# Inverse norm roots as exp(-½ ln x) on ScalarE instead of a ScalarE root and a VectorE reciprocal

## The reference

```python
def rms_norm(x, g):
    xf = x.astype(jnp.float32)
    y = xf * lax.rsqrt(jnp.mean(xf * xf, axis=-1, keepdims=True) + NORM_EPS)
    return (y * g.astype(jnp.float32)).astype(x.dtype)
...
    for layer in range(DEPTH_2):
        x = x + mixers[layer](rms_norm(x, mix_norms[layer]))
        xn, mn, wq, wkv, wo = xattn[layer]
        x = x + memory_cross_attention(rms_norm(x, xn), rms_norm(mem, mn), wq, wkv, wo)
        fn, wg, wu, wd = ffns[layer]
        x = x + swiglu(rms_norm(x, fn), wg, wu, wd)
    return rms_norm(x, final_norm)
```

## Time and profile before

| | |
|---|---|
| median of the runs | 3710.95 us (3707.92 to 3712.61, 3 runs) |
| the profiled execution | 3723.11 us, span 3721.3 us |
| mean granted TensorE clock | 0.921 of full speed |
| PE busy | 3161.6 us, 85% |
| DVE busy | 2067.9 us, 56% |
| POOL busy | 1343.1 us, 36% |
| ACT busy | 715.0 us, 19% |
| DMA | 832.17 MB, 224 GB/s over the span |

### The profile page before, as it was taken

One profiled execution on the slowest core, in us unless ns is written; L12 is line 12 of the kernel. 1 busy time (PEld: TensorE's weight loads), 2 busy tenths in 40 slices (PEclk: granted clock), 3 DMA queues, 4 the chain that ended last, 5 costly groups with the idle time before them and its releaser, 6 DMA issues. The chain is left out here.

```text
span 3721.3 us, 45113 instructions
## 1 busy us (share of the span) xinstructions
PE 3161.6 (85%) x17286; PEld 2328.3 (63%) x17286; DVE 2067.9 (56%) x4210; ACT 715.0 (19%) x1731; POOL 1343.1 (36%) x1166
## 2 busy tenths in 40 slices
PE   8889988976778777567888988889988999999998
PEld 3566378742335343254677766667875788877787
DVE  2341355579898888677776687776444210133201
ACT  2231221121111111113210023210023210122100
POOL 0840032156777777643455555555300000000000
PEclk9998999988889998886899998899999899999999
DMA  6422100379999999976899999899820244422343
GB/s 213 128 74 77 40 3 16 96 273 360 368 364 367 380 385 375 365 260 196 305 333 390 394 369 323 301 351 385 304 82 26 77 133 150 147 91 77 116 147 102
DMA packets 420396, 832.17 MB, mean 224 GB/s; under 512 B 40467, under 2 KB 258510, under 8 KB 420174
## 3 DMA queue, kind: packets, MB, share of 16 engines
q0 software_dynamic: 147456, 536.94, 38.7%
q1 hardware_dynamic: 272726, 292.35, 24.0%
HBM read 827.02 MB, written 2.17 MB: 223 GB/s over the span
## 5 line engine op out<-in xcount | busy, mean ns | idle before, releaser
L2809 PE MATMUL banks<-arena 128*128 128x256 f32 (+1 forms) x4736 | 1079.3, 387 | 76.2 <-DMA arena<-in_l_w_up 27.0
L2809 PEld LDWEIGHTS banks<-arena 128*128 128x128 f32 (+1 forms) x4736 | 911.8, 194 | 229.8 <-issue 41.4
L2356 POOL DMA_INDIRECT arena<-in_peer_v,arena x512 | 584.1, 1141 | 414.4 <-DVE arena L2472 247.7
L2356 POOL DMA_INDIRECT arena<-in_peer_u,arena x512 | 569.9, 1113 | 442.5 <-DVE arena L2486 165.3
L2486 DVE CUSTOM_DVE_ANT_0 arena<-arena 128x1024 f32<-128x1024 f32 x512 | 628.0, 1227 | 109.2 <-DMA arena<-in_peer_u,arena 82.0
L2428 PE MATMUL banks<-arena 128*128 128x512 f32 x768 | 411.3, 678 | 191.0 <-ACT arena L2447 81.5
L2472 DVE SCALAR_TENSOR_TENSOR arena<-arena 128x1024 f32<-128x1024 f32 x316 | 406.3, 1286 | 32.3 <-DMA arena<-in_peer_v,arena 21.2
L2428 PEld LDWEIGHTS banks<-arena 128*128 128x128 f32 x768 | 157.5, 215 | 401.4 <-issue 300.4
L3778 PE MATMUL banks<-arena 128*128 128x256 f32 x1408 | 310.5, 378 | 0.0
L3827 DVE TENSOR_TENSOR arena<-banks,arena 128x512 f32<-128x512 f32 x44 | 30.4, 692 | 497.8 <-PE banks L2809 495.5
L3778 PEld LDWEIGHTS banks<-arena 128*128 128x128 f32 x1408 | 265.7, 189 | 38.3
(11 more groups left out here) (334 smaller groups left out, 3504.9 us busy)
## 6 DMA issues: line engine op xcount, KB each, us to landing
arena<-in_l_w_gate SPq DMA_DIRECT2D x44, 1024.0 KB
arena<-in_l_w_up SPq DMA_DIRECT2D x44, 1024.0 KB
arena<-in_l_w_down SPq DMA_DIRECT2D x44, 1024.0 KB
arena<-in_ada_w SPq DMA_DIRECT2D x24, 1024.0 KB, 7.5
arena<-in_l_w_qkv SPq DMA_DIRECT2D x24, 1024.0 KB
arena<-in_w_in SPq DMA_DIRECT2D x33, 512.0 KB, 4.1
arena<-in_l_w_out SPq DMA_DIRECT2D x16, 1024.0 KB
arena<-in_peer_q_w SPq DMA_DIRECT2D x10, 1024.0 KB
```

The lines of the kernel that those rows point to most:

```text
L2356: p.e.indirect_dma_start(e.ring[slot], None, tables[table], bass.IndirectOffsetOnAxis(ap=e.IDX[h][:, t, j:j + 1], axis=0)).then_inc(*p.up( ...
L2809: ins = p.e.matmul(out, left(c), right(c), start=c == 0, stop=c == c_n - 1, skip_group_check=True)
```

## The change

Every root with its reciprocal becomes a logarithm and an exponential, both on ACT: 1/sqrt(x) = exp(-½ ln x). The new helper `inverse_root` issues Ln (with the scale and the bias that the root had), waits for it by `in_order`, and issues Exp with scale -0.5 on the result.

```diff
+def log_tables(p):
+
+    if not p.counting:
+        p.e.add_instruction(mybir.InstLoadActFuncSet(name=p.e.bass.get_next_instruction_name(), act_func_set_id=LOG_AND_EXP,
+                                                     ins=[], outs=[]))
+
+
+def inverse_root(k, p, out, src, scale, bias, signal, key):
+
+    p.e.activation(out, src, ACT.Ln, scale=scale, bias=bias).then_inc(*p.up(k.S.scalar_step))
+    p.in_order()
+    p.e.activation(out, out, ACT.Exp, scale=-0.5).then_inc(*p.up(signal, key))
...
 def heads_act(k, p):
     S, rw = k.S, k.rw
+    log_tables(p)
     for h in range(2):
         p.wait_ge(S.centred, h)
...
 def norm2_root_act(k, p, h):
     S = k.S
+    if h:
+        log_tables(p)
     p.wait_ge(S.norm_filled, ("norm2", h))
-    p.e.activation(k.rstd[:, half(h)], k.bank[7][:, 0:TH], ACT.Sqrt, scale=1.0 / D, bias=k.EPS).then_inc(
-        *p.up(S.norm_root, ("norm2", h)))
+    inverse_root(k, p, k.rstd[:, half(h)], k.bank[7][:, 0:TH], 1.0 / D, k.EPS, S.norm_root, ("norm2", h))
...
 def scale_act(k, p, a, tag):
     yield 4 * MM
+    if a.h_id == 0 or tag[0] == "l1_mix":
+        log_tables(p)
     p.wait_ge(k.S.norm_filled, tag)
-    p.e.activation(a.r[:, 0, :], k.bank[3][:, 0:TH], ACT.Sqrt, scale=1.0 / D, bias=k.EPS).then_inc(*p.up(k.S.norm_root, tag))
-    if tag[0] in ("x_norm0", "x_norm1", "l1_mix"):
-        exponentials_next(k, p, a)
+    inverse_root(k, p, a.r[:, 0, :], k.bank[3][:, 0:TH], 1.0 / D, k.EPS, k.S.norm_root, tag)
     yield 2000
...
     p.wait_ge(S.norm_root, tag)
     p.in_order()
-    p.e.reciprocal(a.r[:, 0, :], a.r[:, 0, :]).then_inc(*p.up(S.vector_step))
     yield 2000
...
 def latent_act(k, p, a):
     S, h = k.S, a.h_id
     n = TH * (h + 1)
+    if h == 0:
+        log_tables(p)
     p.wait_ge(S.norm_filled, ("latent", h))
     for j, width in enumerate((384, 256)):
-        p.e.activation(a.r[:, j, :], k.bank[6][:, TH * j:TH * j + TH], ACT.Sqrt, scale=1.0 / width, bias=k.EPS).then_inc(
-            *(p.up(S.norm_root, ("latent", h)) if j else p.up(S.scalar_step)))
-    exponentials_next(k, p, a)
+        p.e.activation(a.r[:, j, :], k.bank[6][:, TH * j:TH * j + TH], ACT.Ln, scale=1.0 / width, bias=k.EPS).then_inc(
+            *p.up(S.scalar_step))
+    p.in_order()
+    p.e.activation(a.r, a.r, ACT.Exp, scale=-0.5).then_inc(*p.up(S.norm_root, ("latent", h)))
```

More of the change, by code:

```diff
@@ L444, in prelude_act @@
     p.wait_ge(S.landed("constants"), "rot96")
+    log_tables(p)
     for j, (tag, r, n) in enumerate((("lat", k.rstd, T), ("ctx", k.rstd_ctx, TC))):
         p.wait_ge(S.norm_filled, tag)
-        p.e.activation(r, k.bank[2 + j][:, 0:n], ACT.Sqrt, scale=1.0 / D, bias=k.EPS).then_inc(*p.up(S.norm_root, tag))
+        inverse_root(k, p, r, k.bank[2 + j][:, 0:n], 1.0 / D, k.EPS, S.norm_root, tag)
     for g in range(ADA):
@@ L470, in prelude_dve @@
         p.wait_ge(S.norm_root, tag)
-        p.e.reciprocal(r, r).then_inc(*p.up(S.vector_step))
         p.in_order()
@@ L1232, in rwkv_inputs_act @@
         p.wait_ge(S.keys_filled, g)
-        p.e.activation(rw.sq[:, g, :], k.PS[:, at:at + TK], ACT.Sqrt, bias=k.K["cols"][:, 4:5]).then_inc(*p.up(S.keys_root, g))
+        inverse_root(k, p, rw.sq[:, g, :], k.PS[:, at:at + TK], 1.0, k.K["cols"][:, 4:5], S.keys_root, g)
     yield
@@ L1777, in heads_act @@
         p.wait_ge(S.head_filled, ("spread", h))
-        p.e.activation(rw.o_ra[h], k.bank[6 + h], ACT.Sqrt, scale=1.0 / 64, bias=k.K["cols"][:, 3:4]).then_inc(
-            *p.up(S.spread_root, h))
+        inverse_root(k, p, rw.o_ra[h], k.bank[6 + h], 1.0 / 64, k.K["cols"][:, 3:4], S.spread_root, h)
 def heads_dve(k, p):
@@ L1792, in heads_dve @@
         p.wait_ge(S.spread_root, h)
-        p.e.reciprocal(rw.o_ra[h], rw.o_ra[h]).then_inc(*p.up(S.vector_step))
         p.in_order()
@@ L1891, in norm2_shift_act, with norm2_ready_dve @@
         p.e.activation(x, x, ACT.Identity, bias=k.mod[:, 24 + c, 0:1]).then_inc(*p.up(S.act_scaled, (("norm2", h), c)))
-def norm2_inverse_dve(k, p, h):
-    S = k.S
-    r = k.rstd[:, half(h)]
-    p.wait_ge(S.norm_root, ("norm2", h))
-    p.e.reciprocal(r, r).then_inc(*p.up(S.vector_step))
+def norm2_ready_dve(k, p, h):
+    p.wait_ge(k.S.norm_root, ("norm2", h))
 def norm2_scale_dve(k, p, h):
@@ L1986, in second_half_dve @@
         yield OTHER[2 + i]
-    norm2_inverse_dve(k, p, 1)
+    norm2_ready_dve(k, p, 1)
     yield OTHER[6]
@@ L2690, in beside_act @@
             yield
+        log_tables(p)
         p.wait_ge(S.norm_filled, "mem")
-        p.e.activation(k.mem_r, k.bank[7][:, 0:TC], ACT.Sqrt, scale=1.0 / D, bias=k.EPS).then_inc(*p.up(S.norm_root, "mem"))
+        inverse_root(k, p, k.mem_r, k.bank[7][:, 0:TC], 1.0 / D, k.EPS, S.norm_root, "mem")
     if h in (4, 6):
@@ L2752, in beside_dve @@
         p.wait_ge(S.norm_root, "mem")
-        p.e.reciprocal(k.mem_r, k.mem_r).then_inc(*p.up(S.vector_step))
     if h in (3, 5):
@@ L3580, in latent_dve @@
     p.wait_ge(S.norm_root, ("latent", h))
-    p.e.reciprocal(a.r, a.r).then_inc(*p.up(S.vector_step))
     for c in range(5):
@@ L3986, in out_root_act @@
     tag = "out_norm", a.h_id
+    log_tables(p)
     p.wait_ge(k.S.norm_filled, tag)
-    p.e.activation(a.r[:, j, :], k.bank[b][:, 0:TH], ACT.Sqrt, scale=1.0 / D, bias=k.EPS).then_inc(*p.up(k.S.norm_root, tag))
+    inverse_root(k, p, a.r[:, j, :], k.bank[b][:, 0:TH], 1.0 / D, k.EPS, k.S.norm_root, tag)
 def out_inverse_dve(k, p, a, j):
@@ L3994, in out_inverse_dve @@
     p.in_order()
-    p.e.reciprocal(a.r[:, j, :], a.r[:, j, :]).then_inc(*p.up(k.S.vector_step))
 def out_scale_dve(k, p, a, j, cs):
```

9 lines of the change are left out of this document (4 added, 5 removed).

## The result

The changed kernel took 3676.69 us (median of 8 runs, 3667.66 to 3695.94), the kernel before 3711.7 us beside it (8 runs, 3702.82 to 3720.89). The ratio is 0.9917, 95% interval 0.9900 to 0.9935: some 31 us faster, between 24 and 37 (the medians lie 35 us apart, the means, which the ratio follows, 32). The forecast was 21 us. The profiled execution took 3675.72 us, its span 3673.9 us.

The account below looks back on a forecast made before the run. DMA engines were taken as nearly full from 750 to 2660 us, with norm chains pacing the dips and PE after 2700. Terms 1.3 + 2.74 + 2.74 + 2.74 + 4.6 + 4.5 + 2.74 = 21.4 us off 3710.95 gave 3690; range 3681 to 3702.

Parts of the forecast that it names:

- the five norms: Half 0's norms at about 1829, 1890, 2165, 2368 and 2431 us: 0.7 of 6.5 taken, 4.6 us; ends 0 and 6.5.
- the clock: PE idling less is granted its higher clock sooner: example of larger gains, chance 5%, no term in the sum.
- One norm: A 128x256 norm on the chain: 1.79 us for the reciprocal becomes 0.42 us, gain 1.37 us.
- The loads: Table loads of 1283 ns cost nothing ahead of waits; the attention's start loses one, gain 1.3 us.
- Second norm: First block, both halves: PE, or DVE and POOL, wait for it; 1.37 us each, together 2.74 us.
- final norms: Half 0's, with second block's first norm, on the chain: 2.74 us; half 1's, with the kernel's last norm: 2.74 us.
- latents of half 0: Latent norms where DVE waits for the roots and POOL for DVE: gain 2.74 us.
- Latents of half 1: Scaling starts at 2770.23 rather than 2774.72 us, within PE's 6.07 us of waiting: gain 4.5 us.
- Absorbed by the gathers: Rival: DMA engines nearly full from 750 to 2660 us absorb DVE's savings; 9.9 us left, 3701; chance 15%.
- Slow load: Rival: set 6, never loaded before, loads slowly; 5.1 us eats the gain, 7 us gives 3734; chance 4%.
- slow logarithm: Rival: the logarithm takes its upper end, the reciprocal's 1.753 us; 4 to 7 us gain left, 3705; chance 4%.
- A load put between: Rival: build loads the exponential's own set after the logarithm; 1.30 us on twelve norms, 5.8 left, 3705; chance 2%.

Follow-up runs that it names:

- the reference runs: The kernel before, unchanged, run beside the kernels under test: median 3711.7 us beside the changed kernel's first measurement.
- the control: The kernel before, measured once more with no edit: ratio 1.0014 against the kernel before.
- experiment 11: The changed kernel without the instructions that ask for the table set (`log_tables` returns at once): ratio 0.9985 against the kernel before.
- experiments 4, 5: The kernel before with 20, then 11 products of ones in PE's wait for the latents of half 1: ratios 1.0019 and 1.0018.
- the fillings: The changed kernel with products of ones in PE's waits ahead of two sums, then also behind seven roots of half 0: ratios 0.9899 and 0.9915.

## Why the prediction was wrong

The changed kernel took 3676.7 us; 3690 was forecast, 3681 to 3702 as range. Two steps of the prediction failed: the factor of 0.7 on the five norms, and the clock, which the sum put at nothing. At equal clock it is 26 us faster than the reference runs (30 than the control), against 24.3 us of waiting that is gone; another 15 us less at the low clock (558 to 543, +-6), at 0.27, are 4 us. The 24.3 us are the forecast's 21.4 with 3.6 us more at the five norms and 0.7 less elsewhere; so against the mean of the reference runs, 30.5 us, the five norms miss 3.6 us, the clock 4, and some 2 have no row. Point by point:

- **One norm: right.** 1.37 us forecast, 1.34 measured in PE's waits (4.29 to 2.95, 3.51 to 2.17). Logarithm 474, exponential 417 ns.
- **The loads: right.** All take 1283 ns, no wait begins later for one; the attention's start gains 1.27 us. That the pair must share a set is shown by experiment 11.
- **Second norm, final norms, latents of half 0, last norm, late norms: right** (the table above, 5.5 against 5.7 and so on). From 2946 us to the end PE waits 1.4 us less, nearly all of it at the last norm.
- **Latents of half 1: direct part right, step too small.** 4.43 us against 4.5. But the term had no clock: PE's busy time behind it fell from 148.1 to 140.3 us in the means. That the products right behind the wait ran at half clock because of it is shown (1.8 us; experiments 4, 5); how much of the other 6 us comes from it is not.
- **The five norms: the step that failed.** "But the DMA engines are not idle there ... I take 0.7 of it, 4.6 us." They gave all: PE waits 8.2 us less (+-1.6; 6.5 expected in full), and triple reciprocals cost 0.94 of their length. The times alone would not show it (ratio 0.9999 for the five norms by themselves). A busy share of 81 to 90% did not mean that the chain beside it was covered.
- **The clock: a term left out, the second step that failed.** I had it among the chances at 5%, "as where PE idles for less time and is granted its higher clock sooner", and priced it nowhere; the sum was carried over to the median because "the differences are taken at stages whose pace does not hang on what makes the two differ", and the clock is what makes runs of one kernel differ. The earlier trace rows held the hint: eight products in 3.78 us behind a 6.07 us wait, where ten of the same take 2.43 us ahead of it.
- **The rivals.** Absorbed by the gathers: refuted, the distance grew from 8 us at 1606 to 27.5 at 2703. Slow load, slow logarithm: refuted by the rows. A load put between: not so, but experiment 11 gives what it would leave of the gain, 5.8 us forecast and 5.6 measured (between -1.5 and 13).

What stays open. The five norms came out at 4, and by putting them back at 16 us, at equal clock; half 0 as a whole (13 us) agrees with the waits. The control lies 4 us above the reference runs of the same kernel, and I have no cause. And 2 to 6 us of the gain at equal clock have no row. The 4 us of the clock rest on how the times of many runs go with it, and not on a run in which it alone was changed: the fillings raised it (504 and 518 us at the low level) and no gain could be told.

No version beat the changed kernel: 0.9899 and 0.9915 with fillings, against 0.9917 and 0.9900.

## What to carry to other kernels

Where a root is followed by a reciprocal on DVE and others wait for both, a logarithm and an exponential on ACT save 1.3 us at 128x256, if one table set holds the two and is loaded ahead of the wait; with the build's own loads nearly nothing is left. Take a shortened chain at full length wherever something is seen to wait for it, even beside DMA engines that are 90% busy as here. And look at the length of the matmuls behind a wait: if they are twice their usual, removing the wait pays a second time, where something waits for those matmuls.

## What the hardware showed

- At one place of the program, a 6.1 us wait of PE was followed by products at half clock (3.67 to 3.78 us for 1.99) in seven of seven profiles, and a 12.8 us wait too. A wait of 1.64 us was not (six profiles), nor one of 3.3 us (experiment 11), nor one of 6.1 us filled with other products. This holds for that place: further on in the same stretch the same products behind waits of 0.86 and 2.97 us take anything from 1.99 to 3.78 us, with the old chain and with the new.
- The scatter of runs of one kernel, 0.2%, goes largely with TensorE's granted clock: 59% of its variance in 274 runs.
- Matmuls of ones in a wait raised the clock (0.58 to 0.83, 0.91 to 0.93). In the profile they shortened the place around two sums by 3 us; the timed runs could not tell a gain.
